# Stick-breaking attention: softplus tiles split in two by GpSimd and VectorE, summed by two rounded products in place of one in full precision

## The reference, cut to what matters

```python
def stick_breaking_attention(q, k, v):
    ...
        z = jnp.einsum('bhqd,bhkd->bhqk', qi.astype(jnp.float32), kf) * scale
        q_pos = blk * Q_BLOCK + jnp.arange(Q_BLOCK)
        mask = key_pos[None, :] < q_pos[:, None]
        log_keep = jnp.where(mask, jax.nn.log_sigmoid(-z), 0.0)
        suffix = lax.cumsum(log_keep, axis=3, reverse=True) - log_keep
        a = jnp.where(mask, jnp.exp(jax.nn.log_sigmoid(z) + suffix), 0.0)
        return jnp.einsum('bhqk,bhkd->bhqd', a, vf)
```

## Time and profile before

| | before |
|---|---|
| device time, median of 3 | 4785.92 us (4783.19 to 4791.78) |
| the profiled execution, its own time | 4783.93 us |
| its span | 4782.2 us |
| TensorE busy over the span | 4385.5 us (92%) |
| VectorE, ScalarE, GpSimd busy | 1961.5, 1540.8, 427.5 us |
| the attention stage | about 2301 to 2538 us of the span |

### The profile page before, as it was taken

The page is one execution under the profiler, slowest core; times in us unless marked ns, Lnnn a source line. Parts: engine busy times, 40 slices in busy tenths (PEclk is TensorE's granted clock), DMA queues, the critical chain, the costliest instruction groups (busy, mean ns, idle before and its releaser), DMA issues. The chain is left out here.

```text
span 4782.2 us, 71380 instructions
## 1 busy us (share of the span) xinstructions
PE 4385.5 (92%) x28765; PEld 3553.0 (74%) x28765; DVE 1961.5 (41%) x2942; ACT 1540.8 (32%) x2764; POOL 427.5 (9%) x360
## 2 busy tenths in 40 slices
PE   7988899987979979899998999999989878999998
PEld 5977789856958858677435788888767676888887
DVE  4544426263245552323443434334442363433333
ACT  3732225243233332311575312212332333221221
POOL 0023400010001100012231000000100001000001
PEclk8999999998989999999999999999999889999999
DMA  3110012212110021111000111111111221111112
GB/s 111 39 56 2 2 36 71 51 52 90 44 36 9 9 77 45 62 40 44 31 9 27 44 49 48 48 48 48 52 32 40 55 48 45 49 48 49 48 48 71
DMA packets 340314, 217.22 MB, mean 45 GB/s; under 512 B 22577, under 2 KB 321873, under 8 KB 339938
## 3 DMA queue, kind: packets, MB, share of 16 engines
q1 hardware_dynamic: 340066, 213.67, 15.5%
HBM read 170.99 MB, written 21.76 MB: 40 GB/s over the span
## 5 line engine op out<-in xcount | busy, mean ns | idle before, releaser
L2982 PE MATMUL ffp_acc<-ff_m_hi_rounded,ffp_w_hi_rounded 128*128 128x512 f32 x1024 | 399.8, 390 | 3.3 <-DVE ff_m_rounded L3051 3.3
L2982 PE MATMUL ffp_acc<-ff_m_hi_rounded,ffp_w_rounded 128*128 128x512 f32 x1024 | 399.5, 390 | 0.0
L2982 PE MATMUL ffp_acc<-ff_m_rounded,ffp_w_hi_rounded 128*128 128x512 f32 x1024 | 399.4, 390 | 0.0
L2982 PE MATMUL ffp_acc<-ff_inner_hi_rounded,ffp_w_hi_rounded 128*128 128x512 f32 x1024 | 398.3, 389 | 0.0
L2982 PE MATMUL ffp_acc<-ff_inner_hi_rounded,ffp_w_rounded 128*128 128x512 f32 x1024 | 398.3, 389 | 0.0
L2982 PE MATMUL ffp_acc<-ff_inner_rounded,ffp_w_hi_rounded 128*128 128x512 f32 x1024 | 398.3, 389 | 0.0
L2993 ACT ACTIVATE ffp_w_hi_rounded<-ffp_w 128x256 fp32r<-128x256 f32 x512 | 189.6, 409 | 441.7 <-DMA ffp_w<-w_mlp_dram 218.1
L3047 DVE TENSOR_TENSOR ffp_w_rounded<-ffp_w,ffp_w_hi_rounded 128x256 fp32r<-128x256 f32 x512 | 216.5, 462 | 136.6 <-ACT ffp_w_hi_rounded L2993 132.4
L2982 PEld LDWEIGHTS ffp_acc<-ff_m_hi_rounded,ffp_w_hi_rounded 128*128 128x128 f32 x1024 | 192.9, 188 | 46.7 <-issue 6.4
L2982 PEld LDWEIGHTS ffp_acc<-ff_m_rounded,ffp_w_hi_rounded 128*128 128x128 f32 x1024 | 192.9, 188 | 40.3
L2982 PEld LDWEIGHTS ffp_acc<-ff_m_hi_rounded,ffp_w_rounded 128*128 128x128 f32 x1024 | 192.9, 188 | 40.0
(11 more groups left out here) (598 smaller groups left out, 9935.0 us busy)
## 6 DMA issues: line engine op xcount, KB each, us to landing
ffp_w<-w_mlp_dram SPq DMA_DIRECT2D x256, 128.0 KB, 2.3
ffp_w<-w_up_dram SPq DMA_DIRECT2D x128, 128.0 KB, 2.2
ffp_w<-w_down_dram SPq DMA_DIRECT2D x128, 128.0 KB, 2.3
mid_w<-w_in_dram SPq DMA_DIRECT2D x104, 128.0 KB, 2.7
pa_w<-w_in_dram SPq DMA_DIRECT2D x72, 128.0 KB, 2.7
pb_w<-w_in_dram SPq DMA_DIRECT2D x68, 128.0 KB, 2.6
p1o_w<-w_out_dram SPq DMA_DIRECT2D x32, 256.0 KB, 4.1
mamba_stage<-b_pool SPq DMA_DIRECT2D x9, 896.0 KB, 5.5
```

What stands on the lines that cost most here:

```text
L2982: mm = nc.tensor.matmul(acc[s][:, c, :], rounded(a[:, s, k, :]), rounded(b[:, k, at]), start=(k == 0 and i == 0), stop=(k == KD - 1 and i ...
```

## The change

Each softplus tile is split: GpSimd copies it to `high` with rounding (a new tile, 6 x 512), VectorE subtracts that from `soft` and writes the rounded rest into `ex`, which ScalarE no longer needs then. TensorE multiplies a rounded copy of the triangle (`exact`, whose entries 0 and -1 are exact when rounded; copied once) with `high` and with `ex`, two rounded products in place of the full-precision one. The product with `run` stays as it is.

```diff
+        high = part.sb("high", [P, SL, 512])
+        exact = part.sb("exact", [P, P])
...
             def sums(u):
                 o, _ = span(u)
-                pe.wait_ge(S["soft_done"], u + 1)
-                mm = M(score[:, u % SL, o:], mat("neg_from"), soft[:, u % SL, o:], start=False, stop=True,
-                       skip_group_check=True)
+                pe.wait_ge(S["split"], u + 1)
+                for part_of in (high, ex):
+                    mm = M(score[:, u % SL, o:], rounded(exact[:, :]), rounded(part_of[:, u % SL, o:]), start=False, stop=True,
+                           skip_group_check=True)
...
             scores(0)
             scores(1)
+            pe.wait_ge(S["copied"], 1)
...
         @block.gpsimd
         def _(pool):
+            def round_soft(u):
+                o, _ = span(u)
+                pool.wait_ge(S["soft_done"], u + 1)
+                if u >= SL:
+                    pool.wait_ge(S["summed"], u - SL + 1)
+                nc.gpsimd.tensor_copy(rounded(high[:, u % SL, o:]), soft[:, u % SL, o:]).then_inc(S["rounded"], 1)
+            round_soft(0)
+            round_soft(1)
             for u in range(ALL):
                 e, (o, _) = units[u][3], span(u)
+                if u + 2 < ALL:
+                    round_soft(u + 2)
                 if last(u):
                     continue
-                pool.wait_ge(S["soft_done"], u + 1)
                 pool.wait_ge(S["summed"], u + 1)
...
+            def split_soft(u):
+                o, _ = span(u)
+                dve.wait_ge(S["rounded"], u + 1)
+                T(rounded(ex[:, u % SL, o:]), soft[:, u % SL, o:], rounded(high[:, u % SL, o:]), ALU.subtract).then_inc(S["split"], 1)
+
...
             scale_q(0)
             scale_q(1)
+            V.tensor_copy(rounded(exact[:, :]), mat("neg_from")).then_inc(S["copied"], 1)
             soft_of(0)
             soft_of(1)
+            split_soft(0)
+            split_soft(1)
             for u in range(0, ALL, 2):
                 for w in (u + 2, u + 3):
                     if w < ALL:
                         soft_of(w)
+                for w in (u + 2, u + 3):
+                    if w < ALL:
+                        split_soft(w)
                 mask_of(u)
                 mask_of(u + 1)
```

More of the change, by code:

```diff
@@ L2566, in stick_breaking @@
         S = {n: part.sem(n) for n in (
-            "q_ready", "z_done", "absd", "expd", "logd", "soft_done",
+            "q_ready", "z_done", "absd", "expd", "logd", "soft_done", "rounded", "split", "copied",
             "summed", "weighed", "masked", "run_done", "applied", "out_read", "d")}
```

## The result

The changed kernel takes **4793.6 us** (median of 14 runs, 4789.4 to 4802.8) against 4785.2 us of the kernel before (median of 14, 4781.3 to 4791.8). The ratio is 1.0017, 95% interval 1.0009 to 1.0024: slower by 8.4 us. I forecast 4802 us, +16.6, in a range of 4770 to 4832. So it is slower as forecast, but by half as much, and by less than the 0.2% (9.6 us) that I had set as the line; the interval of the ratio excludes no change all the same.

What follows compares the result with a forecast made beforehand. The prediction took TensorE as the bound before the change and the VectorE-GpSimd loop after it. Three later head pairs at +4.7 us and the first at +2.5 gave +16.6, so 4785.9 + 16.6 = 4802 us, range 4770 to 4832.

Steps and rivals of the forecast that it cites:

- the products' saving: Triangle products on TensorE: two rounded products replace each full-precision one, saving 28 us if TensorE stayed the bound.
- the loop that swallows it: Full steps: chain of VectorE sums and subtractions with GpSimd copies and adds takes 5.5 us where TensorE would need 4.9.
- the hold: VectorE's subtraction waits out GpSimd's add and ends 0.54 us after it; GpSimd's next instruction then waits for VectorE.
- the dear copy: Rival: GpSimd's rounding copy costs what an add does, 0.66 us more per full-width copy; total 4842 us, chance 0.07.
- TensorE was not the bound: Concerns the rival that TensorE stays the bound, with the loop under 4.9 us: 4761 us, chance 0.12.
- its clock did not fall: Concerns the rival that new gaps lower TensorE's clock throughout, full steps needing 9.8 us: near 4890 us, chance 0.03.
- steps 10 to 12: Full 512-column steps ending a head pair: 3 x 5.5 = 16.5 us against 16.04, +0.5 us.
- step 9: Full step of a head pair: 5.5 us plus step 8's masks, 0.5, is 6.0 against 5.48, +0.5 us.
- step 8: 512-column step following a 384 one, with a blocked multiply and two held subtractions: 6.1 us against 5.34, +0.8 us.
- steps 5 to 7: From the end of step 4, with adds, masks and query-tile scaling: 13.3 us against 10.77, +2.5 us.
- change of pair: Three times: output read queued behind two subtractions, about 2.4 us later; cheaper products give back about 2.0: +0.4 us.
- first head pair: About +2.5 us, since it has no change of pair before it and starts at the low clock.

Runs made afterwards that it cites:

- split_alone: Changed kernel with its copies and subtractions kept, but TensorE multiplying the unsplit softplus tile in full precision: stage 251.3 us, median 4806.3 us, ratio 1.0042 to before.
- adds_off_sbuf: Changed kernel with GpSimd's later additions replaced by memsets of the same length, leaving out the running sum: stage 215.3 us, median 4770.0 us.
- the best version: Changed kernel with read-out moved early, copies on VectorE, and in steps 9 to 12 a second softplus sum replacing the copy: 4776.3 us, ratio 0.9980 to before.
- products_alone: Kernel before with a rounded softplus tile multiplied twice, without copies or subtractions, so sums are wrong: stage 208.9 us, median 4762.5 us, ratio 0.9952.
- either reordering of the full steps: Two variants of the changed kernel: VectorE's softplus sums and subtractions interleaved (4795.0 us), or GpSimd's two copies put before its two additions (4794.0 us).

## Why the prediction was right, and where its sizes were off

The mechanism was right; that the time came as near as it did is in part luck, since errors of both signs stood in the sum. Three of the runs show the parts of the mechanism: the products' saving (I forecast 28 us with TensorE as the bound; 25.7 measured), the loop that swallows it (split_alone, where the full steps are those of the changed kernel), and the hold as its cause (adds_off_sbuf). The estimate of GpSimd's copy (0.61 us) met the unheld copies, so the dear copy is excluded; the hold of 0.54 us after the addition was 0.56, where the rule of the Trainium skill that the prediction weighed (SBUF — State Buffer, Who interferes with whom), taken literally, would have 0.69. TensorE was not the bound, and its clock did not fall in the full steps, as the row of steps 9 to 12 of the second pair shows (granted clock 1.00):

```profile
2409.00:2431.30 22.30, 19.60 (x65) 7.38 (x64) 19.42 (x23) 16.51 (x32) 16.30 (x18) 1.00 0.01 1
```

Of the signs that I had named, two came out otherwise: the stage is 245 us long, not 253, and TensorE is busy for 211 us of it, not near 200.

By the terms of the sum, for a later head pair (measured in the second):

| term | forecast | measured |
|---|---|---|
| steps 10 to 12 | +0.5 | 16.51 against 16.04: +0.5 |
| step 9 | +0.5 | 5.77 against 5.48: +0.3 |
| step 8 | +0.8 | 5.98 against 5.34: +0.6 |
| steps 5 to 7 | +2.5 | 10.96 against 10.77: **+0.2** |
| change of pair, end of step 12 to end of the next step 4 | +0.4 | 23.07 against 21.13: **+1.9** |
| sum | +4.7 | +3.5 |
| first head pair | +2.5 | 59.47 against 59.29: +0.2 |

The third pair comes to +3.1 and the fourth to +3.9. They differ from the second in two terms: the change of pair costs +1.5 and +1.3, and in the fourth pair steps 10 to 12 cost +1.5. At its end TensorE has no further scores to form, and steps 11 and 12 of before take 4.64 us each; the changed kernel takes 5.36 and 5.35 as ever, since TensorE isn't its bound there.

**The first term that failed is steps 5 to 7**, as the prediction put it, "step 5 with two adds of 512 behind two short copies 4.0". There are no such additions. Step 4 is the last key tile of its query half, and GpSimd's loop skips the last unit (`if last(u): continue`). The section on the change has the line, and the counts in the earlier trace rows say it too: of the 48 units of 512 columns only 32 have an addition. In the changed kernel GpSimd has no addition between 2389.74 and 2395.17 (its rows there, without the other copies):

```profile
2388.74 1.00 POOL L2695 TENSOR_TENSOR stick_run<-stick_run,stick_soft 128x384 f32<-128x384 f32 x1
2391.35 0.29 POOL L2680 CAST stick_high_rounded<-stick_soft 128x128 fp32r<-128x128 f32 x1 [1.60 <-issue]
...
2395.17 0.46 POOL L2692 TENSOR_TENSOR stick_run<-stick_soft,all_fixed 128x128 f32<-128x128 f32 x1
```

With nothing to hold it, step 5 takes 2.23 us. Steps 5 to 7 together come out 2.3 us shorter than forecast in each of four pairs, and that is the whole of the first pair's miss as well.

**The second is the change of pair.** The place was right: the read-out is queued behind two subtractions, and it came 2.5 us later (idle time 5.18 in place of 2.64; I had 2.4). But I gave back 2.0 us for the cheaper products of steps 2 to 4, "the second of them partly at the low clock", and did not charge the clock for the longer idle time. The four clearing products took 3.78 us at all three changes (2.48, 3.21 and 3.58 before), and the granted clock was 0.54 in the 5 us from 2379 on. Net +1.9, +1.5 and +1.3 in place of three times +0.4: 3.5 us more than forecast.

The errors partly cancel: 4 x 2.3 us too much in steps 5 to 7 and another 1.5 too much in steps 8 and 9; 3.5 too little at the changes of pair, 1.0 in steps 10 to 12 and 0.3 in the first four steps. That leaves +10.7 in the stage for +16.6. The median moved by 8.4; the executions of either kernel spread over more than 10 us, so the 2.3 us between stage and median need no cause of their own.

What stays open: why two of three clearings run at full clock behind 2.24 us of idle time and the third doesn't, and how much of the 15.6 us that are left between the best version and products_alone could be had by moving the masks. No run tries either.

## What to carry to other kernels

Before work is moved from TensorE to VectorE and GpSimd, count how often an instruction with two SBUF operands of the one would start beside an SBUF-reading instruction of the other: here it made the 512-column subtractions 0.9 us longer on average; without the additions' reads the stage was 19.3 us shorter than before, with them 10.7 longer. Where a tile comes from a PSUM operand anyway, forming it a second time from there can be cheaper than copying it in SBUF. And when instructions are put into a queue, look for what stands behind them at the rare places: a read-out three times in the stage was worth more than either reordering of the full steps, and it helped the kernel before as well.

## What the runs showed of the hardware that I had not expected

- VectorE's copy from SBUF to SBUF (512 columns) takes 0.43 us alone and up to 1.27 beside GpSimd's additions. The sum with one operand in PSUM took 0.68 to 0.69 in all of 32 cases, 21 of them beside an addition: longer than the copy alone, but not held.
- The hold costs both sides: GpSimd's copy of 512 columns takes 0.61 us, and 0.96 where it follows a held subtraction; two additions behind each other didn't keep a subtraction from getting in between (3.40 us for 2.54 us of work).
- What TensorE's clock did behind a change of pair could weigh as much as the idle time before it. The same four products took 1.98 or 1.99 us behind 1.14 us of idle time (six times in two kernels) and 3.78 behind 5.18 (three times). In between the idle time alone doesn't order them: 2.98, 1.98 and 2.97 behind 1.52, 1.98, 1.98 and 3.06 behind 2.24, 2.95, 2.92 and 2.85 behind 4.24 (adds_off_sbuf). The granted clock was 1.00 over the first 1.98 behind 2.24, and 0.62 over the 3.06.
